# Gate blocks of seven quarter products in a two-layer diffusion backbone

## The chip, the cores and the metric

The kernel runs on one core of one Trainium2 chip. The metric is the device time of one execution in microseconds (us); lower is better. Five engines work side by side: TensorE (PE in the rows; its weight loads are PEld), VectorE (DVE), ScalarE (ACT), GpSimd (POOL) and SyncE (SP), which here only issues DMAs.

## What is computed

One inference step of two trunk layers on 640 tokens (128 context, 512 latent), all in float32. The part that the change rewrites is the merge gates `mg`, the last 3072 columns of the input projection; most of the rest is around it in time.

```python
h = x * (1 + sc_a) + sh_a                                  # sc_a, sh_a: "modulation" = silu(cond) @ ada_w + ada_b
aq, ak, av, ag, alr_f, alr_b, bz, cq, ck, cv, mg = split_cols(h @ lp["w_in"], IN_WIDTHS)
...                                                        # three mixers: A linear attention, B gMLP, C attention
branches = jnp.stack([br_a, br_b, br_c], axis=2)
proj = jnp.einsum('blnc,ncd->blnd', branches, lp["w_branch"])
gates = jax.nn.sigmoid(mg).reshape(B, L, N_BRANCH, D_MODEL)
y = jnp.sum(gates * proj, axis=2) @ lp["w_out"]
x = layer_norm(alpha * x + gt_a * y, lp["ln1_g"], lp["ln1_b"])
...                                                        # 16 experts, two per token, then a second layer norm
```

## The kernel before, in words

Each engine has its own instruction list, written out by hand, and waits on semaphores. What is shared between engines:

- **PSUM slots.** `build_tables` lists all PSUM results in one order (`jobs`). There are four slots, taken in turn: TensorE may write job n only when job n-4 has been moved out (`wait_slot`). "A" jobs are moved by ScalarE, "D" jobs by VectorE.
- **The ring.** SyncE loads weight blocks of 1 MB (half of that for `wb`) in the order of `blocks` into a ring of six; block n is issued when the last reader of block n-6 is done.

A layer goes: input projections for mixers A and B (jobs `lr, aq, ak, z, vtok, av, ktok, u`), where VectorE works out the decays between the matmuls and must finish the product q, k (`qk_ready`) of step c before ScalarE takes up `z` of step c+1; then the A mixer with the late projections; then 20 **units** u of attention, each of two heads: scores, softmax on ScalarE and VectorE, transposes, values. The merge runs beside the units: 24 steps m, each with a **gate** (an output tile of 128 columns; 8 weight chunks of 128 x 128 by two halves of 320 tokens, so 16 matmuls), a **branch** projection (8 matmuls) and one of the 24 **modulation** blocks b: VectorE forms row sums of a 1 MB `ada` block (`conditioned`, 16 operations on 256 columns), TensorE sums them over the partitions, VectorE adds the bias. Layer 0 has all 24 modulation blocks, layer 1 sixteen. Steps 0 to 11 lie one in a unit, 12 to 15 spread over two units each, 16 to 23 after the units. Beside units 2 and 5 lie the head norms (`head_squares`, `head_roots`, `head_gated`), beside units 0 to 2 the rotations (`swapped`, `rotated`). Then come the output projection, the router and the experts.

In layer 0 GpSimd copies x to the output and fills the buffer `rows` with zeros (two DMAs of 8960 KB) when `ak` is done.

## Time and profile before

| | us |
|---|---|
| median of three runs | 2103.98 |
| lowest and highest | 2101.12, 2105.12 |
| span of the profiled execution, first to last instruction | 2100.0 |
| TensorE busy | 2010.4 (96%) |
| VectorE busy | 964.4 (46%) |
| ScalarE busy | 486.3 (23%) |
| GpSimd busy | 140.3 (7%) |

The timeline gives each instruction's start and length, and in brackets how long its engine had been idle and what it waited for. A matmul stands in the trace as two records, so 16 matmuls read "x32". The view by windows gives the busy time of each engine in a stretch. Of the DMA queues, q1 carries what SyncE issues and q0 what GpSimd issues.

### The profile page before, as it was taken

The page shows a single profiled execution, that of the slowest core. Times are in us where ns is not written, and L with a number is a line of the kernel's source. Part 1 is how long each engine was busy: PE and PEld are TensorE (multiplying, and loading weights), DVE is VectorE, ACT ScalarE, POOL GpSimd, SP SyncE. Part 2 cuts the span into 40 slices and gives each one's busy share as a digit, 9 for nine tenths or more (in the row PEclk, how much of TensorE's full clock was granted, in tenths as well). Part 3 has the DMA queues.
Part 4 walks back from the last instruction along what each step waited for, and adds up shares of the span by engine and source line. Part 5 has one row for each costly group of instructions (what it writes and reads, how often), then busy time and mean ns, then how long its engine had stood idle before and what let it go on. Part 6 is the DMA issues. An engine that isn't in the chain of part 4 may idle for free.

```text
span 2100.0 us, 25029 instructions
## 1 busy us (share of the span) xinstructions
PE 2010.4 (96%) x9957; PEld 1348.4 (64%) x9957; DVE 964.4 (46%) x2068; ACT 486.3 (23%) x778; POOL 140.3 (7%) x198
## 2 busy tenths in 40 slices
PE   6999999999999998999889999999999999999995
PEld 3787776677767786333457877766677677853333
DVE  1136118667766776111172350286677316651116
ACT  1241103433420001111143411134334200101112
POOL 2000000000010003000030000000000000020001
PEclk8999999999999999999999999999999999989998
DMA  9691112324243515998671111124232422369994
GB/s 371 217 333 48 33 51 72 126 90 141 74 163 128 211 54 206 357 365 331 250 267 60 61 50 32 50 73 143 82 133 72 170 81 100 119 229 355 368 341 171
DMA packets 169509, 345.31 MB, mean 164 GB/s; under 512 B 10865, under 2 KB 124081, under 8 KB 159729
## 3 DMA queue, kind: packets, MB, share of 16 engines
q1 hardware_dynamic: 141712, 248.97, 33.5%
q0 software_dynamic: 21024, 72.00, 9.3%
q10 hardware_dynamic: 6656, 22.71, 2.7%
q8 instruction: 83, 1.36, 0.3%
q14 instruction: 34, 0.27, 0.0%
HBM read 286.17 MB, written 60.10 MB: 165 GB/s over the span
## 4 chain that ended last, share of the span: by engine, by line
PE 83%; DMA 8%; DVE 6%; ACT 1%; issue 1%; POOL 1%; SPq 0%; POOLq 0%; DVEq 0%; ACTq 0%
PE PS L1044 78%; DMA store<-in_expert_w_up_dram 4%; PE PS L1048 4%; DMA ar<-in_ada_w_dram 1%; DVE ar L1725 1%; DMA mg<-rows_h,idxi 1%; DMA xr<-out_y_dram 1%; DVE xr L549 1%; ACT store L1514 0%; POOL rows L1016 0%; DMA mg<-rows,posi 0%; DVE store L1725 0%; ACT ar L1514 0%; DMA store<-rows,posi 0%; PE PS L558 0%
## 5 line engine op out<-in xcount | busy, mean ns | idle before, releaser
L1044 PE MATMUL PS<-store 128*128 128x320 f32 (+2 forms) x4192 | 1102.0, 424 | 2.6 <-DVE ar L1725 1.7
L1044 PEld LDWEIGHTS PS<-store 128*128 128x128 f32 (+1 forms) x4192 | 780.7, 189 | 297.1 <-issue 19.1
L1044 PE MATMUL PS<-store,mg 128*64 (+2 forms) x2152 | 499.1, 536 | 22.1 <-DMA store<-in_expert_w_up_dram 12.3
L1044 PEld LDWEIGHTS PS<-store,mg 128*64 128x64 f32 (+1 forms) x2152 | 233.6, 155 | 236.7 <-issue 211.9
L549 DVE SCALAR_TENSOR_TENSOR xr<-store,cs,xr 128x256 f32<-128x256 f32 x560 | 246.7, 482 | 10.0
L1514 ACT ACTIVATE xr<-PS 128x256 f32<-128x256 f32 (+1 forms) x108 | 56.1, 525 | 554.8 <-PE PS L1044 554.8
L1514 ACT ACTIVATE ar<-PS 128x640 f32<-128x640 f32 (+4 forms) x131 | 86.8, 694 | 373.1 <-PE PS L1048 188.9
L1725 DVE TENSOR_TENSOR mg<-PS,mg 128x256 f32<-128x256 f32 x33 | 14.0, 425 | 317.4 <-ACT mg L1514 317.4
L1514 ACT ACT_TABLE_LOAD x112 | 143.7, 1283 | 2.0
L1725 DVE TENSOR_TENSOR ar<-PS,xr 128x640 f32<-128x640 f32 x32 | 26.4, 825 | 153.2 <-PE PS L1044 153.2
L1514 ACT ACTIVATE mg<-PS 128x256 f32<-128x256 f32 x66 | 25.4, 384 | 241.6 <-PE PS L1044 223.3
L1048 PEld LDWEIGHTS PS<-const,mg 128*128 128x128 f32 x386 | 41.5, 140 | 55.0 <-issue 50.3
L1725 DVE TENSOR_TENSOR ar<-PS,const 128x512 f32<-128x512 f32 x32 | 22.1, 690 | 94.2 <-PE PS L1044 93.9
L602 PE MATMUL PS<-const 128*128 128x128 f32 x346 | 51.4, 318 | 10.9 <-ACTq L1711 8.1
L1048 PE MATMUL PS<-const,mg 128*128 128x128 f32 x386 | 57.8, 282 | 4.1 <-DMA mg<-rows_h,idxi 3.8
L978 POOL DMA_DIRECT2D mod_rows<-ar x32 | 17.8, 555 | 651.6 <-DVE store L1922 337.9
L1514 ACT ACTIVATE ar<-ar,sm 128x513 f32<-128x513 f32 (+2 forms) x80 | 55.9, 699 | 12.6 <-DVE sm L1934 12.2
L602 PEld LDWEIGHTS PS<-const 128*128 128x128 f32 x346 | 48.9, 169 | 13.5 <-issue 9.8
L1934 DVE CUSTOM_DVE_ANT_0 ar<-PS,const,sink 128x512 f32<-128x512 f32 (+2 forms) x80 | 56.9, 716 | 0.0
L1514 ACT ACTIVATE store<-PS 128x512 f32<-128x512 f32 (+1 forms) x36 | 22.2, 639 | 125.7 <-PE PS L1044 117.4
L1725 DVE TENSOR_TENSOR mg<-ar 128x640 f32<-128x640 f32 x16 | 12.5, 822 | 76.9 <-ACT er L1514 76.9
L1044 PE MATMUL PS<-ar,store 64*128 64x256 f32 (+1 forms) x352 | 43.6, 369 | 2.9 <-DVE ar L1725 1.6
(249 smaller groups left out, 1408.1 us busy)
## 6 DMA issues: line engine op xcount, KB each, us to landing
store<-in_w_in_dram SPq DMA_DIRECT2D x50, 1024.0 KB, 7.3
store<-in_ada_w_dram SPq DMA_DIRECT2D x43, 1024.0 KB, 5.0
store<-in_expert_w_gate_dram SPq DMA_DIRECT2D x33, 1024.0 KB, 8.5
store<-in_expert_w_up_dram SPq DMA_DIRECT2D x33, 1024.0 KB, 10.8
store<-in_expert_w_down_dram SPq DMA_DIRECT2D x33, 1024.0 KB, 5.6
rows<-const POOLq DMA_DIRECT2D x2, 8960.0 KB, 36.4
rows<-ar ACTq DMA_DIRECT2D x33, 512.0 KB, 8.9
mg<-rows SPq DMA_DIRECT2D x27, 512.0 KB, 11.9
```

The lines of the kernel that those rows point to most:

```text
L549: last = nc.vector.scalar_tensor_tensor(out=out, in0=w[:, k, :], scalar=scalar, in1=out, op0=ALU.mult, op1=ALU.add)
L602: nc.tensor.transpose(ps[:, 0:P], ident, ident)
L978: pool.dma_start(mod_rows[b // 4 - 2, :, 256 * (b % 4):256 * (b % 4 + 1)], staged[b % 2][0:STAGED:GROUP, :]).then_inc(on.mod_staged[b % 2] ...
L1044: return nc.tensor.matmul(out, lhsT, rhs, start=start, stop=stop, skip_group_check=True)
L1048: return nc.tensor.transpose(out, in_, ident[0:n, 0:n])
L1514: return nc.scalar.activation(out, in_, func, **kw)
L1725: return V.tensor_tensor(out, a, b, op)
L1934: moved(V.tensor_tensor_reduce(out=pbuf[i % 4][:, 0:keys], in0=ps[:, 0:keys], in1=mask_of(n), scale=-(HD ** -0.5), scalar=own, op0=ALU.add ...
```

## The change

The eight quarter products of a gate block (2 column tiles by 8 chunks of K in two halves by two token halves) become seven, with sums of quarters of h and of the weights ahead of them and sums of products behind (a Strassen-Winograd scheme). Per pair of gates:

- `weights_summed_first` on GpSimd: two operations on 128 x 512, for the next pair, started when the present pair is filled (one buffer `ws1`); `weights_summed_last` on VectorE: two more, each after the product that reads the quarter that it overwrites.
- `gates` on TensorE: 7 products of 4 matmuls. Three of them are added in PSUM onto a product that ScalarE has copied out before (`kept`).
- `gate_parts` on ScalarE: four copies of 320 columns; `gate_parts_added` on VectorE: four additions of 320 columns; then two sigmoids. The two gate jobs become "D" jobs, both moved by the last addition.
- Once a layer: four sums of quarters of h on VectorE (128 x 1280 each) and two copies on ScalarE.
- Gates now come in pairs: at units 0, 2, 4, 6, 8, 10, 13, 16, 19 and then three after the units; branches 0 to 11 two to a unit at units 1, 3, 5, 7 and 9, and single or after the units from 10 on.
- Head norms move to units 0 and 2, rotations to units 0 (three) and 2 (three); values of the unit before come ahead of the gates.
- The ring is five blocks deep; the sixth place holds the sums. `ada` blocks of steps 4 to 19 stay beside the merge, two to a pair; the first eight blocks of layer 0 are taken in the input projections.

```diff
-RING = 6
+RING = 5
...
+def mods_early(l, after):
+
+    if l == DEPTH - 1:
+        return ()
+    return {("ak", 0): (0,), ("ak", 1): (1,), ("tok", 0): (2,), ("tok", 1): (3,), ("tok", 2): (4,), ("tok", 3): (5,), ("u", 1): (6, 7)}.get(after, ())
...
                     tt(B3, B3, bc(e3[:, 0, :].unsqueeze(2), [P, T, P]), ALU.subtract).then_inc(on.decay_ready, 1)
-                    dve.wait_ge(on.exp_ready, c + 1)
+                    if l < DEPTH - 1:
+                        conditioned(3 + c, first_acc)
+                    dve.wait_ge(on.softplus, 3 * c + 3)
                     tt(mg3[:, c, :], aqk[:, c % 2, :], bufA, ALU.mult)
                     tt(mg3[:, 4 + c, :], aqk[:, 2 + c % 2, :], bufM, ALU.mult).then_inc(on.qk_ready, 1)
-
+                    early(("tok", c))
...
-                    feature_major(("gate", half, n, q), w, h3, slice(P * (q % 2), P * (q % 2) + P))
+                    pair = m // 2
+                    turn1, turn2 = ht12[m // 8 > 0]
+                    x = on.wait_slot(pe, ("gate", half, n, q))
+                    left, right = x[:, 0:HALF], x[:, 512:512 + HALF]
+                    product(left, w[:, 0:4, 0:P], h11, True, True).then_inc(on.product, 1)
+                    product(right, w[:, 4:8, 0:P], h21, True, True).then_inc(on.product, 1)
+                    y = on.wait_slot(pe, ("gate", half, n, q + 1))
+                    low, high = y[:, 0:HALF], y[:, 512:512 + HALF]
+                    pe.wait_ge(on.summed, H_SUMMED)
+                    pe.wait_ge(on.pool_summed, m // 2 + 1)
+                    if m == 8:
+                        pe.wait_ge(on.kept, kept_count(4, 0))
+                    product(low, ws1, turn1, True, True).then_inc(on.product, 1)
+                    product(high, w[:, 4:8, P:2 * P], ht4, True, True)
+                    pe.wait_ge(on.summed, weights_summed(m))
+                    pe.wait_ge(on.kept, kept_count(m, 1))
+                    product(left, w[:, 0:4, 0:P], turn2, False, True).then_inc(on.product, 1)
+                    pe.wait_ge(on.kept, kept_count(m, 2))
+                    product(low, w[:, 4:8, 0:P], h22, False, True)
+                    pe.wait_ge(on.kept, kept_count(m, 3))
+                    product(left, w[:, 0:4, P:2 * P], h12, False, True).then_inc(on.filled, 2)
...
+                def weights_summed_last(m):
+
+                    half, n, q = merge_step(m)
+                    w = on.ring_slot(("mg", half, n, q // 2)).rearrange("p (k c) -> p k c", k=KD)
+                    dve.wait_ge(on.pool_summed, m // 2 + 1)
+                    dve.wait_ge(on.product, 4 * (m // 2) + 1)
+                    step(tt(w[:, 0:4, 0:P], ws1, w[:, 0:4, 0:P], ALU.subtract))
+                    dve.wait_ge(on.product, 4 * (m // 2) + 2)
+                    tt(w[:, 4:8, 0:P], w[:, 4:8, 0:P], w[:, 0:4, 0:P], ALU.subtract).then_inc(on.summed, 1)
...
+                def pair_gated(m):
+
+                    ada, ada1 = mod_beside(m), mod_beside(m + 1)
+                    if ada is not None:
+                        conditioned(ada, acc)
+                    gate_parts_added(m, 0)
+                    if ada1 is not None:
+                        step(row_sums(step, on.wait_block(dve, ("ada", ada1)), acc[ada1 % 2], range(0, KD // 2)))
+                    gate_parts_added(m, 1)
+                    if ada1 is not None:
+                        row_sums(step, on.ring_slot(("ada", ada1)), acc[ada1 % 2], range(KD // 2, KD)).then_inc(on.acc_ready, 1)
...
+                    if gates_beside(u) is not None:
+                        weights_summed_last(gates_beside(u))
                     if u:
                         values_moved(u - 1)
+                    if gates_beside(u) is not None:
+                        pair_gated(gates_beside(u))
+                    for m in branches_beside(u):
+                        gated(m)
```

**TensorE, layer 0, unit 0.** In the kernel before, `ar,store` is a score, `store` 320 wide a gate or a branch, `store,const` 512 wide a rotation:

```order
L1044 MATMUL PS<-ar,store 128x128 [waits act_moved_0,dve_moved_0]
L1044 MATMUL PS<-ar,store 128x128
L1044 MATMUL PS<-store 128x320 [waits dve_moved_0,landed2_0]
L1044 MATMUL PS<-store 128x320 x15
L1044 MATMUL PS<-store,const 128x512 [waits act_moved_0,dve_moved_0]
L1044 MATMUL PS<-store,const 128x512 [waits dve_moved_0]
L1044 MATMUL PS<-store 128x320 [waits dve_moved_0,landed3_0,brb_ready_0]
L1044 MATMUL PS<-store 128x320 x7
```

The same place after, from the head squares (`ar,const`) on:

```order
L1116 MATMUL PS<-ar,const 128x320 [waits dve_moved_0,square_ready_0]
L1116 MATMUL PS<-ar,const 128x320
L1116 MATMUL PS<-ar,const 128x320 [waits act_moved_0,square_ready_0]
L1116 MATMUL PS<-ar,const 128x320
L1116 MATMUL PS<-store,const 128x512 [waits dve_moved_0] x2
L1116 MATMUL PS<-store,const 128x512 [waits act_moved_0,dve_moved_0]
L1116 MATMUL PS<-store 128x320 [waits act_moved_0,landed2_0]
L1116 MATMUL PS<-store 128x320 x7
L1116 MATMUL PS<-mg,store 128x320 [waits pool_summed_0,summed_0,dve_moved_0]
L1116 MATMUL PS<-mg,store 128x320 x3
L1116 MATMUL PS<-store 128x320 x4
L1116 MATMUL PS<-mg,store 128x320 [waits kept_0,summed_0]
```

The gate stood right behind the scores; now two head squares and three rotations stand ahead of it, and the third rotation waits for a ScalarE move.

**VectorE, layer 0, behind the softmax of a unit.** Before (unit 5), one set of row sums, of which the first and the last rows, then the branch's gate:

```order
L1940 TENSOR_SCALAR ar<-ar,sm 128x512 [waits dve_step_0]
L547 TENSOR_SCALAR xr<-store,cs 128x256 [waits landed4_0]
...
L549 SCALAR_TENSOR_TENSOR xr<-store,cs,xr 128x256
L1725 TENSOR_TENSOR mg<-PS,xr 128x640 [waits act_moved_0,filled_0]
L1725 TENSOR_TENSOR ar<-PS,ar 33x256 [waits mod_staged0_0,filled_0]
L1922 COPY store<-PS 128x128 [waits filled_0]
```

After (unit 4, steps 4 and 5):

```order
L2136 TENSOR_SCALAR ar<-ar,sm 128x512 [waits dve_step_0]
L1854 TENSOR_TENSOR store<-store 128x4x128 [waits product_0,pool_summed_0]
L1854 TENSOR_TENSOR store<-store 128x4x128 [waits product_0,dve_step_0]
L2118 COPY store<-PS 128x128 [waits filled_0]
L604 TENSOR_SCALAR xr<-store,cs 128x256 [waits landed2_0]
...
L1854 TENSOR_TENSOR xr<-PS,xr 128x320 [waits kept_0,product_0]
L604 TENSOR_SCALAR xr<-store,cs 128x256 [waits landed3_0]
...
L1854 TENSOR_TENSOR xr<-PS,xr 128x320 [waits kept_0,filled_0,dve_step_0]
L1854 TENSOR_TENSOR xr<-PS,xr 128x320 [waits gate_ready_0]
L1854 TENSOR_TENSOR xr<-PS,xr 128x320
L606 SCALAR_TENSOR_TENSOR xr<-store,cs,xr 128x256 [waits dve_moved_0]
```

One and a half sets of row sums (24 operations) and two weight sums now stand ahead of the additions that free the two gate slots, and half a set behind them.

**SyncE, layer 0, the first blocks.** Before, the loads from the ring's first block on (`in_ada_w` is a modulation block):

```order
L842 DMA store<-in_w_in_dram 128x8x32
L842 DMA store<-in_w_in_dram 128x8x256 x2
L839 DMA const<-in_const_dram 128x3415
L842 DMA store<-in_w_in_dram 128x8x256 x3
L842 DMA store<-in_w_in_dram 128x8x256 [waits filled_0] x9
```

After:

```order
L899 DMA store<-in_w_in_dram 128x8x32
L899 DMA store<-in_w_in_dram 128x8x256 x2
L899 DMA store<-in_ada_w_dram 128x8x256
L896 DMA const<-in_const_dram 128x3415
L899 DMA store<-in_ada_w_dram 128x8x256
L899 DMA store<-in_w_in_dram 128x8x256 [waits filled_0]
L899 DMA store<-in_ada_w_dram 128x8x256 [waits filled_0]
L899 DMA store<-in_w_in_dram 128x8x256 [waits filled_0]
L899 DMA store<-in_ada_w_dram 128x8x256 [waits filled_0]
L899 DMA store<-in_w_in_dram 128x8x256 [waits filled_0]
L899 DMA store<-in_ada_w_dram 128x8x256 [waits filled_0]
L899 DMA store<-in_w_in_dram 128x8x256 [waits filled_0]
```

Eight modulation blocks stand between the projections' blocks, and three fewer projection blocks are loaded ahead.

## Rows read from the trace of the kernel before

**Rows 1.** The page's first part: busy time, share of span, instructions.

```profile
PE 2010.4 (96%) x9957; PEld 1348.4 (64%) x9957; DVE 964.4 (46%) x2068; ACT 486.3 (23%) x778; POOL 140.3 (7%) x198
```

**Rows 2.** Windows: stretch, length, busy PE, PEld, DVE, ACT, POOL, PEclk, DMA, GB/s.

```profile
100.00:153.00 53.00, 53.00 (x247) 45.39 (x246) 18.28 (x27) 23.98 (x39) 2.97 (x1) 1.00 0.96 344
400.00:603.00 203.00, 203.00 (x1130) 143.27 (x1129) 145.25 (x372) 83.51 (x129) 11.16 (x21) 1.00 0.30 101
```

**Rows 3.** PE's timeline, start and length: 32 matmuls in a row, the next work.

```profile
294.19 17.50 PE L1044 MATMUL PS<-store 128*128 128x320 f32 x64
311.52 1.05 PE L1044 MATMUL PS<-ar,xr 128*128 128x128 f32 x8
```

**Rows 4.** Timeline of unit 6, layer 0: transposes before it, scores, row sums, gating.

```profile
415.17 1.09 PE L1048 MATMUL PS<-const,ar 128*128 128x128 f32 x8
...
416.19 1.13 PE L1044 MATMUL PS<-ar,store 64*128 64x256 f32 x8
...
417.26 13.19 PE L1044 MATMUL PS<-store 128*128 128x320 f32 x48
...
420.42 0.61 DVE L547 TENSOR_SCALAR xr<-store,cs 128x256 f32<-128x256 f32 x2
...
421.06 6.38 DVE L549 SCALAR_TENSOR_TENSOR xr<-store,cs,xr 128x256 f32<-128x256 f32 x14
...
430.48 0.82 DVE L1725 TENSOR_TENSOR mg<-PS,xr 128x640 f32<-128x640 f32 x1 [3.04 <-PE PS L1044]
...
431.23 0.41 DVE L1725 TENSOR_TENSOR ar<-PS,ar 33x256 f32<-33x256 f32 x1
```

**Rows 5.** PE's idle gaps beside the merge, layer 0: first, last of five.

```profile
330.01 0.49 PE L1044 MATMUL PS<-ar,store 64*128 64x128 f32 x4 [0.81 <-DVE ar L1725]
...
612.65 4.58 PE L1044 MATMUL PS<-store 128*128 128x320 f32 x16 [0.39 <-DVE store L1922]
```

**Rows 6.** Timeline, head norms: squares at unit 0, roots at unit 2, gating behind.

```profile
313.68 1.36 ACT L1514 ACTIVATE ar<-xr 128x640 f32<-128x640 f32 x2
...
350.53 1.62 ACT L1514 ACTIVATE ar<-PS,const 128x640 f32<-128x640 f32 x2
...
352.17 1.28 ACT L1514 ACT_TABLE_LOAD   x1
353.46 1.36 ACT L1514 ACTIVATE ar<-ar 128x640 f32<-128x640 f32 x2
...
356.60 0.88 DVE L1887 SCALAR_TENSOR_TENSOR xr<-xr,vec,ar 128x640 f32<-128x640 f32 x1
```

**Rows 7.** The page's costliest groups: VectorE on 512 columns, busy, mean ns.

```profile
L1725 DVE TENSOR_TENSOR ar<-PS,const 128x512 f32<-128x512 f32 x32 | 22.1, 690 | 94.2 <-PE PS L1044 93.9
```

**Rows 8.** DMA view of 98 to 114 us: packets, MB, share; a block's landing.

```profile
q0 software_dynamic: 1308, 5.36, 87.8%
q1 hardware_dynamic: 835, 0.86, 15.0%
...
store<-in_w_in_dram SPq DMA_DIRECT2D x1, 1024.0 KB, 19.3
```

**Rows 9.** DMA view of 118 to 122 us, between the two fills.

```profile
q1 hardware_dynamic: 1017, 1.03, 80.5%
```

**Rows 10.** Timeline, input projections of layer 0: z on ScalarE, decay and norms on VectorE.

```profile
103.41 0.79 ACT L1514 ACTIVATE ar<-PS,vec 128x640 f32<-128x640 f32 x1 [1.69 <-DVE mg L1725]
...
110.12 0.83 DVE L1725 TENSOR_TENSOR ar<-ar,er 128x640 f32<-128x640 f32 x1
...
157.84 0.69 DVE L1731 BATCH_NORM_STATS2 st<-xr 128x6 f32<-128x512 f32 x1
...
173.95 0.82 DVE L1725 TENSOR_TENSOR ar<-PS,er 128x640 f32<-128x640 f32 x1
```

**Rows 11.** GpSimd's timeline: its only operation on 128 x 512.

```profile
0.98 0.53 POOL L636 MEMSET w<- 128x512 f32 x1
```

**Rows 12.** Windows, columns as in rows 2: TensorE behind gaps at the layer's end.

```profile
1057.00:1062.00 5.00, 5.00 (x10) 1.98 (x9) 4.50 (x7) 1.53 (x2) 5.00 (x9) 0.67 1.00 393
```

336 lines of the change are left out of this document (228 added, 108 removed).

## The prediction

> **What bounds the kernel now.** The page's first part comes first: TensorE is busy 96% of the span, VectorE 46% [rows 1]. The windows then say where that hides something: beside the merge TensorE runs 203 us of 203 and VectorE is already busy for 145 of them, and in the input projections of layer 0 TensorE has no gap either, but the DMA engines are 0.96 busy [rows 2]. So a matmul removed is worth its full price, and a wait added to TensorE costs its full price too. The gaps beside the merge are few: five in layer 0, from 0.81 down to 0.39 with three of 0.22 between, 1.9 us [rows 5]; layer 1 reads alike. The change takes work from the engine that bounds and hands waits to it; the question is which sum is larger.
>
> **What it removes.** Thirty-two matmuls follow each other in 311.52 - 294.19 = 17.33 us, 0.542 us each [rows 3]. A pair of gates falls from 32 to 28; 12 pairs, two layers, 96 matmuls: **-52.0 us**. The two layers' gaps of rows 5 are replaced by those worked out below: **-3.7 us**. Branches, head squares, rotations and partition sums stay as many as they were and only move.
>
> **The pair in the attention, unit by unit.** Rows 4 give the clock of a unit, t = 0 at its scores (416.19): the gate starts at 1.1 and VectorE is through the softmax at 4.2 (420.42). A set of row sums takes 0.61 + 6.38, 7.0 us. In the new unit the values (about 1 us, as the transposes in rows 4) come first, so the seven products start at 2.05 and end at 2.05 + 28 x 0.542 = 17.2; the transposes end at 18.2, and TensorE wants its next scores. These need both gate slots, which VectorE frees with its last addition. VectorE: first weight sum at 5.0; the second must wait for product two (6.4) and ends at 7.2 (0.69 each, [rows 7]); values moved 7.4; row sums to 14.4; one addition of 320 columns, 0.48, between 0.41 for 256 and 0.82 for 640 [rows 4], to 14.9; half a set, 3.4, to 18.3; three additions with their waits 1.55, to 19.9, some 0.1 for the semaphore. **TensorE idles 1.75 us**; in units of 640 keys its transposes are 0.25 longer, 1.5. Seven such units a layer (4, 6, 16, 19 with 512 keys, 8, 10, 13 with 640): 11.5 us. The cover that is gone: a gate slot was freed by ScalarE alone, long before.
>
> What is queued behind: the second half of the row sums (3.6 us) lies ahead of the next unit's softmax. In units with two branches (about 12 us of TensorE) it is hidden. With one branch (14, 17), softmax 7, gating 0.82 + 0.82, modulation 0.41 end 0.9 us after the transposes: 1.85 together. After branches with two-part gating, VectorE's 0.82 + 0.82 + 0.41 [rows 4] is 0.4 longer than TensorE's partition sums and transposes, since the values no longer stand between; with 640 keys the transposes take up some of it: 0.5 at units 5, 7 and 18, 0.3 at 15, 1.8 us.
>
> **Units 0 and 2.** Rotations are three now, and the third needs slot n-4, a head square that ScalarE must have moved. At unit 0 the squares hold TensorE 1.1 us (ScalarE needs 0.68 each [rows 6] behind the last move). Then exponentials, a table load, logarithms, a table load and a root: from the logarithms' start to the first root 353.46 + 0.68 - 350.53 = 3.6 us [rows 6]. Walked from 313.05, the start of unit 0: exponentials end 317.2, load 1.28, root moved 322.2; rotation two ended at 318.6, so TensorE idles 3.7. VectorE then gates two heads (0.88 + 0.82 each), rotates three (2.07 each) and sums weights, until 333.2, and the fifth product wants that at 331.9: 1.4. The additions cost 1.25 at the end. Together 7.4, and 0.4 behind unit 1. Unit 2 in the same way: rotation five waits 2.5 for the root, the gate's slot waits 2.65 for the first rotation behind two gated heads, additions 1.2, and 0.4 behind unit 3: 6.8. **Sum per layer: 11.5 + 1.85 + 1.8 + 7.8 + 6.8 = 30 us, two layers +60.** The h sums (1.5 us each by length from rows 4 and 7) lie beside the last `cq` projections, 17 us of TensorE: nothing. After the units nothing waits: VectorE has no scores to serve.
>
> **The eight early modulation blocks, layer 0.** With five places, blocks are issued at: `v1` when `ak` ends (81 us, 0.8 later than before), and right with it `ada3` and `av0`. That is when GpSimd starts its copy and fills. While a fill runs, q1 moves 1 KB packets against 4 KB ones, and a block issued at 98 lands after 19.3; the steady part is 0.079 MB/us (0.315 MB in 4 us; 0.86 MB over these 16 us with its start) [rows 8]; between fills 1.03 MB in 4 us [rows 9]. So `v1` lands at 96 as before, `ada3` at about 110, `av0` at 121, `ada4` 126, `av1` 139, `ada5` 153, the rest soon after. VectorE takes `ada3` *before* the product that sets `qk_ready`: row sums until 117, product until 118.7, and the modulation behind it frees the slot of the third `v1` tile, which TensorE wanted at 108.9: **idle 10.1**. `ada4`: decay ready 7.5 after z (103.41 to 110.95 [rows 10]), in time. `ada5` at 153: product at 161.9, third `av1` tile wanted at 157.1: **idle 5.1**. Then `ada6` and `ada7` stand ahead of the norms of v, 16.1 us (157.84 to 173.95 [rows 10]); these end at 202, only then are modulations 6 and 7 moved, and `u2` wants that slot at 196: **idle 6.2**. Sum +21.4. Bounds: nothing, if several transfers outstanding get through at the rate of rows 9; 35, if each takes the 19.3 of rows 8.
>
> TensorE's clock: after gaps of 2 to 4 us the window 1057 to 1062 shows 0.67 granted [rows 12], a mean between the levels 1.2 and 2.4 GHz; that costs 1.7 us. Three long gaps in the projections, so 0 to 5; I take 2.
>
> **GpSimd's sums.** The only row of that size is a memset, 0.53 us [rows 11]; a two-input one on VectorE takes 0.69 [rows 7]. Two per pair cost TensorE nothing by themselves: the next pair's third product is at least 13 us away. Whether they slow VectorE no row shows. They start just as a pair is filled, when VectorE has a microsecond of row sums left before the additions. Bound: nothing to 2 x 0.69 in 14 units, 0 to 19 us; I take nothing, since no row shows VectorE held up by GpSimd.
> The Trainium skill (SBUF — State Buffer, "Who interferes with whom") says that a VectorE operation with two SBUF inputs and a GpSimd operation that reads SBUF exclude each other for a whole instruction. Row sums have two SBUF inputs. By the Trainium skill (GPSIMD Engine Reference, section 3.1, 2.6 cycles an element at 1.2 GHz) one sum would last an estimated 1.1 us; no run here shows it. By the two rules together the total above would be 15 to 30 us larger.
>
> **Sum.** -52.0 - 3.7 + 60 + 21.4 + 2 = **+27.7**, on a span of 2100.0; the median lies 4 us above it. I shade a little, since every wait was walked at its longest: **2129 us**, 1.2% slower.
>
> **The rivals.**
> (a) *GpSimd excludes VectorE*: one operation of 0.69 more before the additions and often a second, +10 to +19: 2139 to 2148. For: the timing of the start. Against: VectorE's additions read PSUM. The rule cited above is this case.
> (b) *The early blocks land in time*: -21 to -23: 2106 to 2108, no change. It decides at whether `ada3` lands before 100 us. Against: rows 8 show 15% for q1.
> (c) *Faster*: VectorE reaches its moves before TensorE asks. The place is the last addition of a pair and the root at units 0 and 2. If the walk is long by one softmax stage at each (the row sums fit under products six and seven, the exponentials end earlier), 12 to 20 us of the 30 a layer go: 2129 - 2 x 16 = 2097, to 2085 when (b) joins. It decides at 17 us of waits a layer: below that the 56 us saved win against 21 + 2. For: VectorE's work in two units (row sums 14.0, gating 3.3, additions and weight sums 3.3, modulation 0.8, softmax and values about 7) is 28 of TensorE's 31.5 us. Against: it fits only if nothing is waited for.
> That fewer matmuls run is certain from the instruction order.
>
> **How the numbers follow.** Forecast 0.45, (a) 0.22, (b) 0.10, (c) 0.23. A measurement here tells about 0.2%, 4 us, from no change. Slower: 0.67; same 0.10; faster 0.23. The range takes in most of (a) and the nearer part of (c): 2090 to 2148.
>
> **What would show it.** Right: TensorE busy 50 us less; at the transposes of units 4, 6, 8, 10 scores that waited 1.5 to 1.75 us for VectorE's 320-wide addition; at unit 0 a rotation that waited 3 to 4 us for ScalarE; in layer 0 gaps of about 10, 5 and 6 us between 105 and 205 us, with q1 at 15 to 22% during the fills; layer 1's projections unchanged. Wrong: row sums without gaps but longer than 7.0 us (a); no gap before 120 us (b); scores that wait under 0.7 us (c).

## The result

The changed kernel takes 2172.4 us (median of four, 2171.9 to 2173.1), the kernel before 2104.6 beside it: ratio 1.032, 95% interval 1.0307 to 1.0341. It is 3.2% slower. The forecast was slower, at 2129, with a range up to 2148; the direction was right, the size 43 us short.

The page of the changed kernel, first part, to be set beside [rows 1]; its profiled span is 2170.0:

```profile
PE 1986.8 (92%) x9765; PEld 1328.7 (61%) x9765; DVE 1071.2 (49%) x2220; ACT 490.1 (23%) x846; POOL 206.5 (10%) x246
```

There are 192 records fewer (96 matmuls), and yet the busy time is only 23.6 us less instead of 52.0: matmuls ran slower than before, by some 28 us. The idle time of TensorE is 183.2 instead of 89.6 us, 93.6 more. Most of both lies beside the merge and in the first projections. This table is read from TensorE's timeline, each stage from the first matmul of its kind to that of the next (*projections*: from `lr` to the first scores; *attention*: to the first output projection; *rest*: output projection, router, experts):

| us | projections 0 | attention 0 | rest 0 | projections 1 | attention 1 | rest 1 |
|---|---|---|---|---|---|---|
| before | 271.9 | 402.6 | 367.4 | 272.4 | 396.5 | 348.0 |
| changed | 295.4 | 423.4 | 366.3 | 272.5 | 419.0 | 352.8 |

**A pair of gates, unit 4 of layer 0** (timeline, to be set beside [rows 4]):

```profile
415.82 1.13 PE L1116 MATMUL PS<-ar,store 64*128 64x256 f32 x8 [0.79 <-DVE mg L1854]
...
423.39 6.38 DVE L606 SCALAR_TENSOR_TENSOR xr<-store,cs,xr 128x256 f32<-128x256 f32 x14
...
429.68 0.48 DVE L1854 TENSOR_TENSOR xr<-PS,xr 128x320 f32<-128x320 f32 x1
430.08 0.60 DVE L604 TENSOR_SCALAR xr<-store,cs 128x256 f32<-128x256 f32 x2
430.73 3.72 DVE L606 SCALAR_TENSOR_TENSOR xr<-store,cs,xr 128x256 f32<-128x256 f32 x6
...
432.43 1.04 PE L1120 MATMUL PS<-const,ar 128*128 128x128 f32 x8
...
432.74 1.42 POOL L1036 TENSOR_TENSOR store<-store 128x512 f32<-128x512 f32 x1 [26.66 <-PE PS L1116]
434.13 1.45 POOL L1037 TENSOR_TENSOR store<-store 128x512 f32<-128x512 f32 x1
434.48 1.41 DVE L1854 TENSOR_TENSOR xr<-PS,xr 128x320 f32<-128x320 f32 x3
...
436.15 1.13 PE L1116 MATMUL PS<-ar,store 64*128 64x256 f32 x8 [2.68 <-DVE xr L1854]
...
437.21 1.69 PE L1116 MATMUL PS<-ar 128*64 128x128 f32 x16
...
438.83 5.61 PE L1116 MATMUL PS<-store 128*128 128x320 f32 x16
```

The last of the six row sums by itself (VectorE alone, 433.05 to 434.4 us):

```profile
432.96 1.49 DVE L606 SCALAR_TENSOR_TENSOR xr<-store,cs,xr 128x256 f32<-128x256 f32 x1
```

Three things are to be seen. The scores wait 2.68 us for VectorE's last addition, where 1.75 was forecast. Six row sums, with no gap between them, take 3.72 us, 1.0 more than 6 of the 14 above (6.38 x 6/14 = 2.73). The whole loss is in the last of the six: it alone takes 1.49 us where the others take 0.48, it starts within GpSimd's first sum and ends 0.3 us behind it. The three additions, which read PSUM, stand beside GpSimd's second sum and keep their length. And the work behind the gap is slow: 1.69 us for the values (x16), which take 1.09 elsewhere, 5.61 for sixteen records of a branch that take 4.57. The windows show the clock there (columns as in [rows 2]):

```profile
400.00:603.00 203.00, 185.84 (x977) 131.60 (x976) 147.30 (x362) 70.56 (x125) 26.93 (x30) 0.97 0.29 93
437.00:445.00 8.00, 8.00 (x41) 5.11 (x37) 6.08 (x18) 3.18 (x6) 0.00 (x0) 0.79 0.01 3
```

**Units 0 and 19**: the third rotation waits for ScalarE's root, and at the end of unit 19 the values and the next branch wait for VectorE.

```profile
345.28 1.94 PE L1116 MATMUL PS<-store,const 128*128 128x512 f32 x2 [3.76 <-ACT ar L1620]
347.01 5.37 PE L1116 MATMUL PS<-store 128*128 128x320 f32 x16
...
668.90 1.29 PE L1116 MATMUL PS<-ar 128*64 128x128 f32 x16 [3.82 <-DVE xr L1854]
672.78 6.39 PE L1116 MATMUL PS<-store 128*128 128x320 f32 x16 [2.59 <-DVE store L2118]
```

**Projections of layer 0**: the gaps behind the early modulation blocks, and VectorE's wait for the first of these.

```profile
107.39 0.61 DVE L604 TENSOR_SCALAR store<-store,cs 128x256 f32<-128x256 f32 x2 [11.75 <-DMA store<-in_ada_w_dram]
...
116.01 12.63 PE L1116 MATMUL PS<-store 128*128 128x256 f32 x48 [7.76 <-DVE mod L621]
...
156.89 10.63 PE L1116 MATMUL PS<-store 128*128 128x256 f32 x48 [0.63 <-DVE mod L621]
...
194.37 5.96 PE L1116 MATMUL PS<-store 128*128 128x320 f32 x15 [4.07 <-DVE mod L621]
```

### The profile page after: what moved, and what is told of

The parts are those of the page before. It is cut to its first block, busy times and chain, and to the rows that moved or that the text cites. A ratio compares the mean times of both kernels' runs of the same rounds, so it can differ in the third digit from the quotient of the medians.

```text
span 2170.0 us, 25058 instructions
## 1 busy us (share of the span) xinstructions
PE 1986.8 (92%) x9765; PEld 1328.7 (61%) x9765; DVE 1071.2 (49%) x2220; ACT 490.1 (23%) x846; POOL 206.5 (10%) x246
## 4 chain that ended last, share of the span: by engine, by line
PE 66%; DVE 18%; DMA 10%; issue 2%; ACT 2%; POOL 1%; SPq 0%; POOLq 0%; DVEq 0%; ACTq 0%
PE PS L1116 63%; DVE xr L606 6%; DMA store<-in_expert_w_up_dram 5%; PE PS L1120 2%; DMA store<-in_ada_w_dram 2%; DVE ar L1854 2%; DVE xr L1854 2%; DMA ar<-in_ada_w_dram 1%; DVE store L606 1%; DMA mg<-rows_h,idxi 1%; ACT ar L1620 1%; DVE mg L1854 1%; DVE store L1854 1%; DVE xr L604 1%; DMA store<-rows,posi 1%
## 5 line engine op out<-in xcount | busy, mean ns | idle before, releaser
L1116 PE MATMUL PS<-store 128*128 128x320 f32 (+2 forms) x3616 | 973.1, 429 | 24.3 <-DVE mod L621 12.4
L1116 PEld LDWEIGHTS PS<-store 128*128 128x128 f32 (+1 forms) x3616 | 680.7, 192 | 285.6 <-issue 44.2
L606 DVE SCALAR_TENSOR_TENSOR xr<-store,cs,xr 128x256 f32<-128x256 f32 x448 | 214.5, 520 | 9.7
L1620 ACT ACTIVATE xr<-PS 128x320 f32<-128x320 f32 (+1 forms) x156 | 64.2, 416 | 590.3 <-PE PS L1116 590.2
L1036 POOL TENSOR_TENSOR store<-store 128x512 f32<-128x512 f32 x24 | 32.4, 1349 | 545.5 <-PE PS L1120 285.5
L1854 DVE TENSOR_TENSOR xr<-PS,xr 128x320 f32<-128x320 f32 x96 | 44.7, 486 | 71.8 <-PE PS L1116 70.4
L1116 PE MATMUL PS<-xr,store 128*128 128x320 f32 x256 | 74.1, 432 | 0.0
L1116 PEld LDWEIGHTS PS<-ar,store 64*128 64x128 f32 x352 | 34.7, 194 | 56.7 <-DVE xr L1854 40.4
L1116 PEld LDWEIGHTS PS<-xr,store 128*128 128x128 f32 x256 | 48.6, 190 | 20.3
## 6 DMA issues: line engine op xcount, KB each, us to landing
mg<-rows SPq DMA_DIRECT2D x27, 512.0 KB, 12.5
```

The source lines that it names most:

```text
L606: last = nc.vector.scalar_tensor_tensor(out=out, in0=w[:, k, :], scalar=scalar, in1=out, op0=ALU.mult, op1=ALU.add)
L1036: nc.gpsimd.tensor_tensor(ws1, w[:, 0:4, P:2 * P], w[:, 4:8, P:2 * P], ALU.add)
L1116: return nc.tensor.matmul(out, lhsT, rhs, start=start, stop=stop, skip_group_check=True)
L1620: return nc.scalar.activation(out, in_, func, **kw)
L1854: return V.tensor_tensor(out, a, b, op)
```

## Experiments

In each, the edit is to the changed kernel unless said otherwise. The theory has three parts: GpSimd's sums hold VectorE, a longer gap costs a slower clock as well, and VectorE's load (row sums above all) makes the additions late. Each run stands beside its own measurement of the kernel before; these read 2103.1 to 2105.4 us, so 2 us between two runs say nothing. "The attentions" are the two stages of the table above, layer 0 first.

### GpSimd's sums cut short

```diff
+                    k, c = (4, P) if m == 0 else (1, 8)
-                    nc.gpsimd.tensor_tensor(ws1, w[:, 0:4, P:2 * P], w[:, 4:8, P:2 * P], ALU.add)
+                    nc.gpsimd.tensor_tensor(ws1[:, 0:k, 0:c], w[:, 0:k, P:P + c], w[:, 4:4 + k, P:P + c], ALU.add)
...
```

> The changed kernel, with GpSimd's two sums of weight quarters cut from 128 x 512 to 128 x 8 (but for the first pair of a layer): work is left out, and the gates of the later pairs are not the reference's. All waits stay. In the changed kernel the half set of row sums ahead of the additions took 3.72 us where its length without a gap would be 2.73, while two GpSimd sums of 1.42 and 1.45 us ran beside it. Theory (GpSimd holds VectorE up): that half set goes back to 2.7 to 2.8 us in 14 units, the scores behind wait about 1.6 instead of 2.6 us, 14 us less; and since gaps of 1.5 us in that trace had no slow matmuls behind them, most of the 1.6 us a unit that the transposes and branches lose behind the gap come back too: 2136 to 2158, from 2172. Rival (the forecast's value for this term, nothing): row sums and gaps as they are, 2170 to 2174.

Measured 2145.3 us, 27 less. The attentions take 408.6 and 408.2 us, 14.8 and 10.8 less. Unit 4:

```profile
432.25 2.71 DVE L606 SCALAR_TENSOR_TENSOR xr<-store,cs,xr 128x256 f32<-128x256 f32 x6
...
434.26 0.36 POOL L1037 TENSOR_TENSOR store<-store 128x8 f32<-128x8 f32 x1 [28.80 <-PE PS L1117]
...
436.67 1.13 PE L1117 MATMUL PS<-ar,store 64*128 64x256 f32 x8 [1.68 <-DVE xr L1855]
```

The row sums are back to 2.71 us, and the scores wait 1.68; the units of 640 keys read 1.54, 1.45 and 1.45. That is the walk of the prediction (1.75 and 1.5) to a tenth, once nothing holds VectorE. The first part of the theory stands. By the two traces the 24.5 us between the profiled executions are 14.8 us of idle time and 9.8 us of busy time: behind none of the twelve shorter gaps at units 4 to 16 is the granted clock lower.

### GpSimd's sums at another moment

```diff
-                    if m:
+                    beside = [u for u in range(UNITS // 2 - 1) if m and gates_beside(u) == m - 2]
+                    if beside:
+                        on.wait_moved(pool, ("s", 2 * beside[0] + 3))
+                    elif m:
                         on.wait_filled(pool, ("gate",) + merge_step(m - 1))
```

> The changed kernel, with GpSimd's two sums for the next pair started when the scores of the following unit have been moved (VectorE then waits for ScalarE's exponentials), instead of when the present pair is filled; nothing left out. The kernel with the sums cut short took 2145.3 us, 27 less than the changed kernel. Theory (it is the moment of the sums that costs, since VectorE is held for each while the additions are due): half sets of row sums back to 2.7 us, scores waiting 1.5 to 1.7 us, 2145 to 2152. Rival (the exclusion costs the same wherever the sums lie, because VectorE is loaded over both units): row sums whole, but softmax or gating later by 1 us and more a pair, 2160 to 2172.

Measured 2157.9, between the two: 14.5 of the 27 us. The additions are free (scores wait 1.71 at unit 4), but VectorE's scaling of the softmax is now held, each of two from 0.49 to over 1.3 us:

```profile
440.34 1.27 POOL L1039 TENSOR_TENSOR store<-store 128x512 f32<-128x512 f32 x1 [31.25 <-DVE sm L2133]
441.56 1.46 POOL L1040 TENSOR_TENSOR store<-store 128x512 f32<-128x512 f32 x1
...
440.55 1.35 DVE L2139 TENSOR_SCALAR ar<-ar,sm 128x512 f32<-128x512 f32 x1
...
442.00 1.31 DVE L2139 TENSOR_SCALAR ar<-ar,sm 128x512 f32<-128x512 f32 x1
```

Each scaling ends 0.3 us behind the sum that runs beside it. VectorE now loses 1.7 us a pair instead of 1.0, but at a place where TensorE feels less of it; some comes back as longer waits for the gating (1.30 us behind unit 14 and 1.41 behind unit 17, where the changed kernel had 0.52 and 0.74).

### The same gap filled with matmuls

```diff
+                    if u >= 4 and gates_beside(u) is not None:
+                        on.wait_moved(pe, ("pT", 2 * u))
+                        for _ in range(5):
+                            mm(on.slot(("pT", 2 * u))[:, 704:704 + HALF], ident, h11[:, 0, :], True, True)
```

> The changed kernel, with five more matmuls of 128x320 (2.7 us at the full clock, results unused) behind the transposes of units 4, 6, 8, 10, 13, 16 and 19, just where TensorE idles 2.6 us: they replace idling by work of the same length, so by themselves they give nothing back. Theory (the idle time lowers the granted clock of what follows): the four matmuls' transposes and branches behind them run at their usual pace (x16 transposes and values 1.1 instead of 1.7 us, x16 matmuls 4.6 instead of 5.6), 14 x 1.6 = 22 us less: about 2150 (2145 to 2158). Rival (the matmuls behind the gap are slow for another reason, contention for memory with VectorE or GpSimd): still slow behind, 2170 to 2180.

Measured 2163.2, 9 less; the attentions 417.2 and 418.1, 7.1 less together. Unit 4 and the windows behind it:

```profile
435.47 2.96 PE L1116 MATMUL PS<-store,const 128*128 128x320 f32 x10 [0.25 <-ACT ar L1624]
438.36 1.14 PE L1116 MATMUL PS<-ar,store 64*128 64x256 f32 x8
439.43 1.09 PE L1116 MATMUL PS<-ar 128*64 128x128 f32 x16
440.45 4.57 PE L1116 MATMUL PS<-store 128*128 128x320 f32 x16
```
```profile
437.00:446.00 9.00, 9.00 (x52) 5.74 (x51) 8.04 (x23) 4.40 (x8) 0.34 (x1) 1.00 0.22 75
```

More matmuls made the kernel faster. Nothing behind is slow, and the granted clock is 1.00 where it was 0.79, though VectorE and GpSimd work as before. The size was wrong. With the filler the scores start 4.18 us (512 keys) or 4.39 us (640 keys) behind the start of the transposes and not 3.72, which is 6.5 us in the twelve units 4 to 16; and of the twelve gaps of the changed kernel there only seven had slow work behind them. So these gaps cost some 13 to 14 us of clock (7.1 + 6.5), not 22. The changed kernel's trace agrees: behind those seven gaps TensorE is busy for 26.7 us at half the clock, which is 13.4 us lost.

### Gaps put into the kernel before

```diff
                         moved(f(pTbuf[i % 4][:, 0:keys], ps[:, 0:keys], ACT.Copy))
+                    if 5 <= u < 19:
+                        for _ in range((0, 2, 4, 7, 10)[(u - 5) % 5]):
+                            step(f(idle_out[:, :], const[:, 0:8], ACT.Copy))
+                        act.sem_inc(on.held, 1)
...
+                    if 6 <= u < 20:
+                        pe.wait_ge(on.held, u - 5)
```

> The kernel before, with TensorE held at the start of units 6 to 19 until ScalarE has moved the second transpose of the unit before and then done 0, 2, 4, 7 or 10 operations on 8 columns (their results are unused): idle gaps of about 0.7, 1.2, 1.8, 2.6 and 3.4 us in turn, 28 in the two layers, in a kernel that has none there; nothing else is changed. What the idle time itself costs is then the sum of the gaps, about 28 x 1.9 = 54 us less what VectorE's slack hides. Theory of the clock (gaps of 2.4 us and more are followed by matmuls at a lower granted clock, those of 1.5 us and less are not): the 16 matmuls behind the two longest gaps take 5.4 to 6.4 us instead of 8.7 x 16/32 = 4.4 to 4.6 in at least half of the cases, 11 to 20 us in all on top of the gaps: 2165 to 2180. Rival (the slow matmuls of the changed kernel come from something else of the change): the same gaps with no slow matmul behind, 2150 to 2160.

Measured 2168.8 against 2105.4: 63 us more. The gaps came out at nothing (no added operation), 1.1 to 1.2, 1.6 to 1.7, 2.3 to 2.4 and 3.1 us; the 22 of them are 43.6 us of idle time. The attentions grew by 29.2 and 32.5, so 18 us lie in slower matmuls. One of each kind, and windows behind them:

```profile
451.92 1.36 PE L1046 MATMUL PS<-ar,store 64*128 64x256 f32 x12 [1.60 <-ACTq L1647]
453.20 13.19 PE L1046 MATMUL PS<-store 128*128 128x320 f32 x48
...
471.63 1.36 PE L1046 MATMUL PS<-ar,store 64*128 64x256 f32 x12 [2.42 <-ACTq L1647]
472.92 13.19 PE L1046 MATMUL PS<-store 128*128 128x320 f32 x48
...
492.29 2.50 PE L1046 MATMUL PS<-ar,store 64*128 64x256 f32 x12 [3.14 <-ACTq L1647]
494.72 14.87 PE L1046 MATMUL PS<-store 128*128 128x320 f32 x48
```
```profile
452.00:460.00 8.00, 8.00 (x37) 5.85 (x38) 6.29 (x18) 4.27 (x6) 0.53 (x1) 1.00 0.58 206
472.00:480.00 8.00, 8.00 (x38) 5.78 (x35) 6.53 (x19) 3.99 (x6) 0.54 (x1) 1.00 0.03 4
492.00:500.00 8.00, 7.71 (x25) 5.40 (x26) 4.80 (x15) 4.55 (x7) 0.54 (x1) 0.62 0.39 130
```

Behind the twelve gaps up to 1.7 us nothing was slow; behind the six of 2.3 to 2.4 three times; behind the four of 3.1 each time. A slow stretch cost 1.6 to 3.2 us, about as much as the gap itself. 0.62 is a mean of 1.2 and 2.4 GHz. Nothing of the change is in this kernel, so idle time alone brings the slow matmuls, and not something else of the change.

### Row sums all behind the additions, and row sums left out

```diff
                     gate_parts_added(m, 0)
-                    if ada1 is not None:
-                        step(row_sums(step, on.wait_block(dve, ("ada", ada1)), acc[ada1 % 2], range(0, KD // 2)))
                     gate_parts_added(m, 1)
                     if ada1 is not None:
-                        row_sums(step, on.ring_slot(("ada", ada1)), acc[ada1 % 2], range(KD // 2, KD)).then_inc(on.acc_ready, 1)
+                        conditioned(ada1, acc)
```

> The changed kernel, with the whole second set of row sums of a pair behind the four additions instead of half of it ahead; nothing left out. Theory (the additions that free the gates' slots come late because row sums stand ahead of them, and a gap of 2.6 us costs TensorE another 1.6 us at a lower granted clock behind it): the waits of the scores at units 4, 6, 8, 10, 13, 16 and 19 fall from 2.6 to under 0.6 us and the slow stretch behind them goes, 14 x (2.1 to 4.2) = 29 to 59 us less, minus up to 14 us because the softmax of the next unit starts 3.5 us later: 2113 to 2150. Rival (VectorE is the bound over two units, so that a wait only moves): new waits of 2 to 3 us at the transposes or the gate slots of the next unit, 2165 to 2175.

Measured 2197.8, 25 *more*: the rival's mechanism, and past its range. The scores behind unit 4 now wait 0.83 us, but the next unit pays: its partition sums wait for the softmax, and its branch is then slow; at the end of unit 19 the next branch waits for the values, which stand behind a whole set of row sums.

```profile
445.12 0.62 PE L1116 MATMUL PS<-xr,const 128*32 128x256 f32 x4 [1.89 <-DVE sm L2128]
445.94 6.24 PE L1116 MATMUL PS<-store 128*128 128x320 f32 x16 [0.20 <-DVE sm L2128]
...
684.84 6.59 PE L1116 MATMUL PS<-store 128*128 128x320 f32 x16 [7.04 <-DVE store L2116]
```

The counterpart cuts the second set to its first chunk and leaves the order:

```diff
-                        step(row_sums(step, on.wait_block(dve, ("ada", ada1)), acc[ada1 % 2], range(0, KD // 2)))
+                        row_sums(step, on.wait_block(dve, ("ada", ada1)), acc[ada1 % 2], range(0, 1)).then_inc(on.acc_ready, 1)
                     gate_parts_added(m, 1)
-                    if ada1 is not None:
-                        row_sums(step, on.ring_slot(("ada", ada1)), acc[ada1 % 2], range(KD // 2, KD)).then_inc(on.acc_ready, 1)
```

> The changed kernel, with the second set of row sums of each pair cut to the first of its eight chunks, ahead of the additions (0.9 instead of 7 us); work is left out, and half of the later modulations are not the reference's. GpSimd's sums stay where they are. Theory (VectorE's load of two sets of row sums a pair sets the waits): the scores behind the pairs wait 0.8 us or less in place of 2.6, no slow matmuls behind them, the wait of the values at the end of unit 19 falls too: 14 x (1.8 + 1.0) + 2 x 3 = 45 us less, 2127 (2120 to 2136). Rival (the chain of additions behind the last product and the end of GpSimd's sum set the wait, not the row sums): waits of 1.5 to 2 us stay, 2145 to 2155.

Measured 2110.6, 62 less; 46.5 of it in the attentions (397.1 and 398.8), as expected. Another 14 are in the experts of layer 0 (352.5 instead of 366.3): with other modulations the tokens can be routed otherwise, and that part says nothing. At the pairs with row sums the scores wait 0.83 or 0.61 us; at units 0 and 2, which have none, they wait 1.49 as in the changed kernel. So the waits come from VectorE's load over two units, and putting the row sums behind the additions only moves them. The 46.5 us hold the cost of GpSimd's sums too, since a row sum that is left out cannot be held; the two experiments do not add up.

### Zero fills spread, norms and rotations apart

```diff
-                    for at in (0, half):
-                        pool.dma_start(pieces[:, at:at + half, :], ...)
...
                 for b in range(MOD_FIRST, MOD_ALL):
+                    if l == 0 and b < MOD_FIRST + 14:
+                        at = piece * (b - MOD_FIRST)
+                        pool.dma_start(pieces[:, at:at + piece, :], ...)
```

> The changed kernel, with the two zero fills of 8960 KB in layer 0 taken out of the input projections and given as 14 pieces of 1280 KB beside the modulation blocks of the merge; nothing left out. Theory (ada3 and ada5 land late because the fills leave the load queue 15 to 22% of the DMA time): the landings of the early blocks fall under 10 us, the TensorE gaps of 7.8 and 4.1 us in 105 to 205 us go, with the slow matmuls behind them 2.1 and 1.8 us: 14 to 17 us less, 2155 to 2160. Rival (the fills' bytes cost the same wherever they lie): the gaps move to the attention of layer 0, where a ring block lands too late, 2168 to 2175.

Measured 2160.1, 12 less, at the edge of what was expected, and projections 0 take 283.8 instead of 295.4. Between 98 and 114 us a modulation block now lands in 5.0 us (23.9 in the changed kernel), and up to 180 us TensorE has no gap. Left is one long gap, of 3.56 us at 182.41 (4.07 before the edit): modulations 6 and 7 stand behind the norms of v, and these did not get faster with the DMA.

```diff
-    return {0: (0, 1, 2), 2: (3, 4, 5)}.get(u, ())
+    return {1: (0, 1, 2), 3: (3, 4, 5)}.get(u, ())
```

The same run puts `weights_summed_last` ahead of `head_gated` in VectorE's list.

> The changed kernel, with the six rotations taken out of units 0 and 2 and put, three each, into units 1 and 3, and with VectorE's two weight sums ahead of the head gatings; head norms stay at units 0 and 2; nothing left out. Theory (at units 0 and 2 the head norms' roots stand ahead of the rotations and of the weight sums, so TensorE waits; 13.6 us of gaps in units 0 to 3 of layer 0 and some 3 us of slow matmuls behind them, layer 1 alike): the waits of 3.76 and 2.40 us for ScalarE and of 1.5 to 1.8 us for VectorE go, about 10 us a layer: 2148 to 2156. Rival (the work is only moved: the rotations at units 1 and 3 make VectorE late for the two branches there): new waits of 2 to 3 us in units 1 and 3, 2162 to 2174.

Measured 2153.5, 19 less (attentions 413.1 and 411.5). The waits of 3.76 and 2.40 for ScalarE are gone; a new one of 1.6 stands in each of units 1 and 3, behind a rotation.

### One addition earlier

```diff
-                    product(low, w[:, 4:8, 0:P], h22, False, True)
+                    product(low, w[:, 4:8, 0:P], h22, False, True).then_inc(on.product, 1)
...
-                    f(sig[1][:, 0:HALF], x[:, 0:HALF], ACT.Copy).then_inc(on.gate_ready, 1)
+                    f(sig[1][:, 0:HALF], y[:, 512:512 + HALF], ACT.Copy).then_inc(on.gate_ready, 1)
...
-                    on.wait_filled(dve, ("gate", half, n, q + 1))
+                    dve.wait_ge(on.product, 5 * pair + 5)
                     dve.wait_ge(on.kept, kept_count(m, 3))
                     tt(sig[0][:, HALF:TOK], y[:, 0:HALF], sig[0][:, HALF:TOK], ALU.add).then_inc(on.gate_ready, 1)
+                    on.wait_filled(dve, ("gate", half, n, q + 1))
```

> The changed kernel, with one addition of a pair put behind product six instead of behind the last one, and ScalarE's fourth copy taken from product four, so that two additions of 320 columns (1.0 us) instead of three (1.5) and no ScalarE copy stand between the last product and the free gate slots; nothing left out. Theory (VectorE's chain behind the last product sets the wait of the scores): 0.5 us less at each of 18 pairs in the units, and a part of the slow matmuls behind where the wait falls from 2.6 to 2.1: 10 to 18 us less, 2154 to 2162. Rival (VectorE comes to the additions late because of row sums held up by GpSimd, so that all four still stand behind the last product): the waits stay 2.4 to 2.7 us in the pairs with row sums, and only units 0 and 2 gain 0.5 us each, 2 us in all: 2168 to 2172.

Measured 2172.9: nothing, the rival. In unit 4 a row sum held by GpSimd lasts until 433.3 us, so the three additions still come behind the last product, and the scores wait 2.76; where there are no row sums the wait fell from 1.49 to 0.96.

### Together

The five moves are the three above (fills, norms, GpSimd's moment) and, of the row sums and of unit 19:

```diff
-                        step(row_sums(step, ..., acc[ada1 % 2], range(0, KD // 2)))
+                        step(row_sums(step, ..., acc[ada1 % 2], range(0, 2)))
                     gate_parts_added(m, 1)
+                    if m == MERGE_LATE:
+                        values_moved(UNITS // 2 - 1)
```

> The changed kernel with five moves together, nothing left out: rotations at units 1 and 3 with the weight sums first; the zero fills in 14 pieces beside the merge; GpSimd's sums at the next unit's softmax; two of eight chunks of the second set of row sums ahead of the additions instead of four; at unit 19 the values moved ahead of the rest of the row sums. If the terms found so far add up: norms 20, fills 12, GpSimd 20 to 25, the shorter wait of the scores 14 x 0.8 = 11, unit 19 2 x 4 = 8, together 71 to 76 less than 2172: about 2098 (2088 to 2112), no slower than the kernel before at 2103. If VectorE is the bound over two units (the kernel with all of the second set behind was 25 us slower), the split and GpSimd's sums give little: 2118 to 2130.

Measured 2124.3, 48 less instead of 71 to 76. At units 11, 14 and 17, with one branch each, the transposes now wait 1.0 to 1.35 us twice, for the softmax and for the values behind it. At the pairs with row sums the scores wait 0.7 to 0.9 us.

```diff
-        for c in rot_beside(u):
-            job("D", "rot", c)
         if u:
             job("D", "pv", u - 1)
+        for c in rot_beside(u):
+            job("D", "rot", c)
```

The lists of TensorE and VectorE change in the same way, and the edit of *One addition earlier* is taken in.

> The kernel with five moves (2124 us), and two more, nothing left out: one addition behind product six (as in the run beside it), and at units 1 and 3 the rotations behind the values of the unit before, so that the branch's slot no longer waits for a rotation (1.6 us each, four in all). Theory (the remaining gaps are worth their length): 14 x 0.5 + 4 x 0.5 for the additions and 6 for the rotations, 12 to 15 us less: 2109 to 2113. If VectorE is the bound in the pairs with row sums, only the rotations and units 0 and 2 count, 8 us: 2116.

Measured 2118.0, 6 less, near the 8 that were expected if VectorE is the bound. The earlier addition did pay here, where it had paid nothing in the changed kernel: at the pairs with row sums the scores wait 0.31 us instead of 0.7 to 0.9. The rotations' part was lost: at units 1 and 3 the branch waited 1.5 and 1.9 us for the values behind the softmax, as long as for a rotation before.

```diff
-    return MOD_FIRST + m - MOD_FROM if MOD_FROM <= m < MOD_FROM + MOD_ALL - MOD_FIRST else None
+    if MOD_FROM <= m < 12:
+        return MOD_FIRST + m - MOD_FROM
+    return m if m >= MERGE_LATE else None
```

GpSimd's order of sums and stores follows it, here and in the next run.

> The kernel with seven moves, and the row sums of units 13 and 16 (modulation blocks of steps 12 to 15) moved to steps 20 to 23 behind the units, where VectorE has no scores to serve; nothing left out. In the kernel with five moves units 11, 14 and 17, each with one branch, had transposes that waited 1.25 and 1.0 to 1.35 us for the softmax, with slow matmuls behind. Theory (VectorE's load in the units is the bound): the waits at units 13, 14, 16 and 17 go, about 4 x 1.5 us a layer, 10 to 14 us less than the kernel with seven moves: 2096 to 2103, faster than the kernel before by a little or equal. Rival (the last modulation now comes late, and with it the gain rows of the first layer norm): the output projection's rows wait, 2112 to 2125.

Measured 2132.6. The attentions fell to 385.0 and 386.2, 14 and 13 us, as the theory has it; but the gain rows are late, as the rival had it and by more than its range, and the output projection waits:

```profile
741.60 3.78 PE L1126 MATMUL PS<-store,mg 128*128 128x256 f32 x8 [19.84 <-DVE ar L1863]
```

```diff
+    steps = tuple(range(MOD_FROM, 12)) + (12, 14) + tuple(range(MERGE_LATE, MERGE_LATE + 6))
+    return MOD_FIRST + steps.index(m) if m in steps else None
```

> The kernel with seven moves, with the 16 later modulation blocks at steps 4 to 11, 12, 14 and 16 to 21 (two sets of row sums at units 4, 6, 8, 10 and 19, one at 13 and 16, two pairs behind the units), and the zero fills in 10 pieces instead of 14; nothing left out. With the last modulation at step 23 the attentions took 385 and 386 us instead of 399, but the output projection waited 20 us for the rows made of it; step 21 lies one pair, 24 us, earlier. Theory (load on VectorE in the units): attentions of 386 to 389 us each and no wait in the output projection: 2094 to 2098, 0.3 to 0.5% faster than the kernel before. Rival (the rows are late still, or one set each at units 13 and 16 is enough for the waits): 2104 to 2116.

Measured 2091.6 (ratio to the kernel before 0.994, 0.9922 to 0.9958), 2 us better than the best expected; the attentions take 388.7 and 387.9, and the 19.84 us are gone.

```diff
+                    if u:
+                        values_moved(u - 1)
                     for i in both:
                         keys = keys_of(i // HEADS)
                         dve.wait_ge(on.exp_done, i + 1)
...
-                    if u:
-                        values_moved(u - 1)
```

> The kernel of the run beside it (modulations spread), with VectorE's copy of the values of the unit before taken while it waits for the exponentials, and not behind the softmax; nothing left out. Theory: waits of 1.5 and 1.9 us at units 1 and 3, and of 1.0 at the transposes of the single-branch units, all for this copy, go, some 5 to 6 us a layer: 2083 to 2089, 0.7 to 1.0% faster than the kernel before. Rival (the next wait of the same unit, for the softmax, takes their place): within 3 us of the run beside it.

Measured 2080.8: ratio 0.989, 95% interval 0.9872 to 0.9908, **1.1% faster than the kernel before** with nothing left out, and again 2 us better than the best expected. Its page and unit 4:

```profile
PE 1965.3 (95%) x9765; PEld 1320.6 (64%) x9765; DVE 1064.7 (51%) x2220; ACT 487.5 (23%) x846; POOL 207.0 (10%) x254
```
```profile
406.83 0.49 DVE L1857 TENSOR_TENSOR xr<-PS,xr 128x320 f32<-128x320 f32 x1
...
409.16 1.13 PE L1120 MATMUL PS<-ar,store 64*128 64x256 f32 x8 [0.31 <-DVE xr L1857]
```

TensorE is 45 us less busy than before, of the 52 that the seven products should save. Against the kernel before, the attentions are 20.4 and 14.2 us shorter. Projections 0 are still 12.0 longer; some 7 of it are the eight moved partition sums (0.95 us each, 0.8 to 0.9 from one to the next matmul), which the attention no longer has. Rest 1 is 5.1 longer. The moves alone could not have given this to the kernel before, which idles only 1.9 us beside the merge of a layer.

## Why the prediction was right or wrong

The direction was right, and so was most of the walk through the units. Two steps failed: GpSimd's sums were put at nothing, and the lower clock behind gaps beside the merge had no price.

**Matmuls removed, -52.0: right.** 96 are fewer, and in the last run, where the clock is full beside the merge, 45 us of it show.

**The clock, +2: the largest error by terms.** The step read [rows 12] as a matter of three long gaps in the projections and priced none beside the merge. Busy time fell by 23.6 instead of 52, so slower matmuls cost about 28 us. In the changed kernel's trace 13 to 14 lie behind the additions' gaps at units 4 to 16, some 8 at units 0 and 2, some 4 at unit 19 and some 4 in layer 0's projections (x48 in 12.63 us for 10.5; the rest behind 4.07). The price per gap was in the sum (1.7 us). The prediction wrote down waits of 3.7, 2.5 and 2.65 us at units 0 and 2 and did not charge it for them. For its gaps of 1.5 and 1.75 us nothing was due, as the run with GpSimd's sums cut short shows; these had to be paid for only because GpSimd made them longer.

**GpSimd's sums, 0: wrong, rival (a) in part.** GpSimd's first sum holds VectorE's last row sum before the additions for 1.0 us in every unit with row sums. With what hangs on it (a gap of 2.68 us instead of 1.7 can have slow work behind it) it is 27 us, above the 10 to 19 of rival (a). Rival (a) rightly said that the additions read PSUM; they were not held, the row sum ahead of them was. The absence of a row was taken for evidence of no hold. It was none, since beside the merge of the kernel before GpSimd only issues DMAs. The exclusion that the Trainium skill states (SBUF — State Buffer, "Who interferes with whom") agrees with this trace, by the 3.72 against 2.71 us. The estimate of 1.1 us a sum (GPSIMD Engine Reference, section 3.1) is low: a sum takes 1.26 to 1.28 us where no row sum stands beside it and 1.42 to 1.45 where one does. The 15 to 30 us that the prediction worked out from the two rules, and did not use, take in the 27.

**Waits of the units, 30 a layer: right by its steps, 39.5 and 38.1 measured.** Without GpSimd's sums the scores wait 1.68 and 1.45 to 1.54 us for a forecast of 1.75 and 1.5; unit 0's root costs 3.76 for 3.7; units 0 to 3 together 13.6 for 14.6. The weight sums' 1.4 at unit 0 did not come, since the matmuls ahead were slow: in the run with the gap filled, layer 1, they happened to run at the full clock, and the wait is there, 1.11 us. Missing were 7 x 1.0 for GpSimd, and unit 19: it was walked like the others, but there the values, and with them the next branch, are queued behind the rest of the row sums: 3.82 + 2.59 us in layer 0, 2.57 + 2.79 in layer 1, for 1.75.

**Early blocks, +21.4: too high, and near the total by luck.** Projections 0 grew 23.5 us; about 7 are moved partition sums, some 4 the clock, and only 12.5 the gaps that the term stands for: 7.76, 0.63 and 4.07 for 10.1, 5.1 and 6.2. The first block landed at 107 and not 110, the third at 148 and not 153. The cause was right for the first two (with the fills spread there is no gap up to 180 us), and for the third, which stays at 3.56 us then, it was the order behind the norms of v, as predicted. Rival (b) is out.

**Rival (c)** asked for waits under 17 us a layer, and that VectorE reach its moves in time. The kernel as changed had 39.5 and 38.1; with row sums, rotations, values and GpSimd's sums placed anew the waits are 12 us a layer, and the time is 2080.8. The rival's own sum was off: 2097 less the 21 of (b) is 2076, not 2085.

**The sum, redone** on the profiled executions (70.0 more, 42.3 above the 27.7 of the sum): 26 for busy time beyond the 2 priced, 18 for idle time beside the merge (39.5 + 38.1 - 60), less 9 in the first projections, 6 of idle time in rest 1 (38.2 instead of 32.1 us, with the stretch behind the last matmul), and 1 elsewhere. By causes instead of by kinds, and roughly: GpSimd's hold 27 (1.0 us of idle time at each of 14 pairs, and the clock behind these gaps), unit 19's queue 10 with its clock, the clock at units 0 and 2 and in the projections 10 beyond the 2 priced, rest 1 6, less the 9.

Rest 1 had no term at all. TensorE waits there 8.3 us for the experts' weights instead of 4.5. The stage is 4.8 us longer in the changed kernel and 1 to 7.6 longer in those derived from it (25 in the run where the gain rows came late); but it is 1.8 longer as well in the kernel before with gaps put in. The ring of five places is a rival that no run tried; against it stands that rest 0 is not longer. Its cause stays open. That the predicted time was shaded 3 us below its own sum went the wrong way too.

## What to carry to other kernels

Taking matmuls from the bound engine paid here only when the engine that is given the additions had time to spare over the whole period, and not at one point. Count its work over two or three steps, and test the count by leaving work out. A gap in TensorE had a second price behind it once it was long enough (never up to 1.7 us, in half the cases at 2.3 to 2.4, each time at 3.1), so fourteen waits cut from 2.6 to 1.6 us returned twice their length. A term with no row in the kernel before is not a term of nothing: GpSimd's sums had none, since no such work ran there. Work given to GpSimd counts on VectorE too wherever it holds VectorE: another moment chose another step to be held, and gave back 14.5 of 27 us.
